# Feed-forward projections of a float32 transformer block with high and low input side by side in one 512-column operand

## What is computed

```python
def conv_ffn(x, w_up, conv_w, conv_b, w_down):      # x 256 x 1024, w_up 1024 x 5632, w_down 2816 x 1024
    u = x @ w_up
    ...
    up = jnp.pad(u, ((0, 0), (half, half), (0, 0)))
    c = conv_b
    for j in range(CONV_W):                          # CONV_W = 3, half = 1
        c = c + conv_w[j] * up[:, j:j + s]
    g, val = c[..., :FFN_HIDDEN], c[..., FFN_HIDDEN:]
    return (jax.nn.gelu(g) * val) @ w_down
```

## Time and profile before

| | |
|---|---|
| Median of 3 runs | 1061.26 us (1060.95 to 1061.63) |
| Profiled execution | span of 1058.9 us from the first to the last instruction |
| Busy over the span | TensorE 97%, VectorE 63%, ScalarE 53%, GpSimd 39% |
| Chain that ended last | TensorE 89% of the span, VectorE 4%, GpSimd 2%, ScalarE 2% |
| Two feed-forwards | 127.44 to 306.00 us and 451.04 to 626.68 us |

### The profile page before, as it was taken

How to read it: one execution, slowest core, us unless ns; L and a number is a source line. 1 busy time by engine, 2 the same in 40 slices (tenths; PEclk the granted TensorE clock), 3 DMA queues, 4 the chain that set the end, 5 groups by cost and what they waited for, 6 DMA issues and landing times.

```text
span 1058.9 us, 21783 instructions
## 1 busy us (share of the span) xinstructions
PE 1032.1 (97%) x8214; PEld 948.2 (90%) x8214; DVE 669.7 (63%) x1102; ACT 556.9 (53%) x1010; POOL 414.2 (39%) x281
## 2 busy tenths in 40 slices
PE   9899999999999999899999999999999999999997
PEld 7799699999988998699999997899999999999996
DVE  4555767677666666776776756766676555554445
ACT  5455665555555554756555566644443355554443
POOL 1000234433352334334333454865754375533331
PEclk9999999999999999999999999999999999999999
DMA  8333466665543544266656534233213244446551
GB/s 327 122 116 129 134 216 187 197 196 173 172 173 104 162 134 144 98 217 196 198 178 205 171 102 158 102 121 114 87 61 120 81 138 152 150 138 217 190 179 48
DMA packets 45993, 161.75 MB, mean 153 GB/s; under 512 B 5233, under 2 KB 5489, under 8 KB 45809
## 3 DMA queue, kind: packets, MB, share of 16 engines
q1 hardware_dynamic: 44784, 156.79, 45.3%
q0 software_dynamic: 1152, 4.19, 1.2%
HBM read 159.91 MB, written 1.05 MB: 152 GB/s over the span
## 4 chain that ended last, share of the span: by engine, by line
PE 89%; DVE 4%; POOL 2%; ACT 2%; issue 1%; DMA 1%; DVEq 0%; SPq 0%; ACTq 0%
PE work L400 14%; PE work L402 14%; PE work L401 14%; PE work L1777 9%; PE acc L400 6%; PE acc L401 6%; PE acc L402 5%; PE work L2499 4%; PE work L2511 3%; PE acc L2511 2%; POOL low L369 1%; PE acc L2028 1%; PE acc L2042 1%; PE acc L2044 1%; PE work L992 1%
## 5 line engine op out<-in xcount | busy, mean ns | idle before, releaser
L369 DVE TENSOR_TENSOR low<-raw,high 128x1024 fp32r<-128x1024 f32 (+2 forms) x185 | 273.7, 1487 | 160.9 <-ACT high L357 160.7
L369 POOL TENSOR_TENSOR low<-raw,high 128x1024 fp32r<-128x1024 f32 x108 | 263.1, 2440 | 286.1 <-ACT high L357 283.6
L357 ACT ACTIVATE high<-raw 128x1024 fp32r<-128x1024 f32 (+2 forms) x293 | 299.7, 1031 | 41.4 <-DMA raw<-in_w_out 25.0
L400 PE MATMUL work<-xh,high 128*128 128x256 f32 (+1 forms) x1032 | 289.9, 281 | 1.8 <-DVE v_sb L1469 1.7
L401 PE MATMUL work<-xl,high 128*128 128x256 f32 (+1 forms) x1032 | 287.9, 279 | 0.0
L402 PE MATMUL work<-xh,low 128*128 128x256 f32 (+1 forms) x1032 | 287.8, 279 | 0.0
L400 PEld LDWEIGHTS work<-xh,high 128*128 128x128 f32 (+1 forms) x1032 | 193.2, 187 | 8.7 <-issue 6.6
L401 PEld LDWEIGHTS work<-xl,high 128*128 128x128 f32 (+1 forms) x1032 | 193.3, 187 | 1.7
L402 PEld LDWEIGHTS work<-xh,low 128*128 128x128 f32 (+1 forms) x1032 | 193.3, 187 | 0.2
L1227 POOL TENSOR_TENSOR h<-gelu,cv 128x256 f32<-128x256 f32 x44 | 50.6, 1149 | 198.7 <-ACT gelu L1148 87.9
L1777 PE MATMUL work<-xh,high 128*128 128x256 f32 x256 | 76.7, 300 | 0.0
(11 more groups left out here) (393 smaller groups left out, 2197.3 us busy)
## 6 DMA issues: line engine op xcount, KB each, us to landing
raw<-in_w_ffn SPq DMA_DIRECT2D x132, 512.0 KB, 4.3
raw<-in_w_out SPq DMA_DIRECT2D x39, 512.0 KB, 4.1
raw<-in_w_att SPq DMA_DIRECT2D x32, 512.0 KB, 4.0
raw<-in_w_diff SPq DMA_DIRECT2D x31, 512.0 KB, 4.3
raw<-in_w_gdn SPq DMA_DIRECT2D x24, 512.0 KB, 4.0
raw<-in_w_mla SPq DMA_DIRECT2D x8, 512.0 KB, 3.6
raw<-in_w_gdnz SPq DMA_DIRECT2D x8, 512.0 KB, 3.6
raw<-in_w_mla SPq DMA_DIRECT2D x8, 384.0 KB, 3.1
```

What stands on the lines that cost most here:

```text
L357: act.activation(high[k][:, 0:w], raw[k][:, 0:w], ACT.Copy).then_inc(high_done[k], 1)
L369: eng.tensor_tensor(low[k][:, 0:w], raw[k][:, 0:w], high[k][:, 0:w], ALU.subtract).then_inc(low_done[k], 1)
L400: pe.matmul(out, lhs[0], rhs[0], start=start, stop=False)
```

## The change

The two input tensors become one, `xx`, with `xh` and `xl` as its halves. In the feed-forward's projections the two matmuls with the high weights become one of 512 columns, which writes high x high into columns 0 to 255 of a bank and high x low into columns 256 to 511; the matmul with the low weights adds to the first half. The two halves of a bank then have to be summed: ScalarE copies the second half to a new tile (`up_g` or `up_v`), VectorE adds the first half to it, and the middle tap and the outer taps read that sum from SBUF instead of PSUM. TensorE may write a bank again after the sum, no longer after the last tap. The high and low parts of slots 0, 1 and 2 move behind the copy and the sum of the bank that follows; that of slot 3 keeps its place. Other stages are as before, except for the counts of the semaphores that they share.

```diff
-    xh = sb("xh", [P, KB, TOK], F32R)
-    xl = sb("xl", [P, KB, TOK], F32R)
+    xx = sb("xx", [P, 2, KB, TOK], F32R)
+    xh, xl = xx[:, 0], xx[:, 1]
...
+    def project_pair(pe, bank, k, blocks=KB, arriving=None):
+
+        for b in range(blocks):
+            if arriving is not None and b % 4 == 0:
+                pe.wait_ge(n_["xl"], 4 * arriving + 2 + b // 2)
+            hi, lo = wslot(k, b * P, b * P + P)
+            pe.matmul(bank, hi, xx[:, :, b, :], start=(b == 0), stop=False)
+            last = pe.matmul(bank[:, 0:TOK], lo, xh[:, b, :], start=False, stop=(b == blocks - 1))
+        return last
...
-                    pe.wait_ge(f[j]["g_tap"] if gate else f[j]["v_tap"], 2 * (i + done))
+                    pe.wait_ge(f[j]["g_sum_tap"] if gate else f[j]["v_sum_tap"], 3 * (i + done) - 2)
...
-                project_t(pe, W[bank][:, 0:TOK], bank, arriving=2 * layer + 1 if first else None).then_inc(used[bank], 1)
+                project_pair(pe, W[bank], bank, arriving=2 * layer + 1 if first else None).then_inc(used[bank], 1)
...
                 act.wait_ge(used[bank], p.base[bank] + i + 1)
+                if not (isinstance(i, int) and i + done == 0):
+                    act.wait_ge(summed, 3 * (i + done))
+                act.activation(u[:], W[bank][:, TOK:2 * TOK], ACT.Copy).then_inc(made, 1)
+                if bank and not (late and value):
+                    refill(split, p, bank - 1, i)
+                act.wait_ge(summed, 3 * (i + done) + 1)
                 if value and not (isinstance(i, int) and i + done == 0):
                     act.wait_ge(s["h32"], i + done)
-                act.activation((cg, cv)[value][j][:], W[bank][:, 0:TOK], ACT.Identity,
+                act.activation((cg, cv)[value][j][:], u[:], ACT.Identity,
                                scale=ffn_taps(layer, i, j, value, 1, 0),
-                               bias=ffn_taps(layer, i, j, value, 3, 0)).then_inc((s["g_mid"], s["v_mid"])[value], 1)
-                if not late:
+                               bias=ffn_taps(layer, i, j, value, 3, 0)).then_inc(made, 1)
+                if bank == 3 and not late:
                     refill(split, p, bank, i)
...
-                dve.wait_ge(mid, i + done + 1)
-                dve.scalar_tensor_tensor(c[:, 1:TOK], W[bank][:, 0:TOK - 1], ffn_taps(layer, i, j, value, 0, 0),
+                dve.wait_ge(mid, 2 * (i + done) + 1)
+                dve.tensor_tensor(u[:], W[bank][:, 0:TOK], u[:], ALU.add).then_inc(tap, 1)
+                if bank and not (bank == 3 and last_step):
+                    refill(split, p, bank - 1, i)
+                dve.wait_ge(mid, 2 * (i + done) + 2)
+                dve.scalar_tensor_tensor(c[:, 1:TOK], u[:, 0:TOK - 1], ffn_taps(layer, i, j, value, 0, 0),
                                          c[:, 1:TOK], ALU.mult, ALU.add).then_inc(tap, 1)
...
-                if not (j and last_step):
-                    refill(split, p, bank, i)
```

More of the change, by code:

```diff
@@ L1081, in mla_dve @@
         over(dve, HEADS, head, 2)
-    f = [sems(f"f{j}", "g_mid v_mid g_tap v_tap gelu h32 hh hl") for j in range(2)]
+    f = [sems(f"f{j}", "g_copy_mid v_copy_mid g_sum_tap v_sum_tap gelu h32 hh hl") for j in range(2)]
+    up_g = [sb(f"up_g{j}", [P, TOK]) for j in range(2)]
+    up_v = [sb(f"up_v{j}", [P, TOK]) for j in range(2)]
     cg = [sb(f"cg{j}", [P, TOK]) for j in range(2)]
@@ L1138, in block @@
                 bank, s = 2 * j + value, f[j]
+                u = (up_g, up_v)[value][j]
+                made, summed = (s["g_copy_mid"], s["v_copy_mid"])[value], (s["g_sum_tap"], s["v_sum_tap"])[value]
                 act.wait_ge(used[bank], p.base[bank] + i + 1)
+                if not (isinstance(i, int) and i + done == 0):
[4 more added lines that the diff above has]
+                act.wait_ge(summed, 3 * (i + done) + 1)
                 if value and not (isinstance(i, int) and i + done == 0):
                     act.wait_ge(s["h32"], i + done)
-                act.activation((cg, cv)[value][j][:], W[bank][:, 0:TOK], ACT.Identity,
+                act.activation((cg, cv)[value][j][:], u[:], ACT.Identity,
                                scale=ffn_taps(layer, i, j, value, 1, 0),
-                               bias=ffn_taps(layer, i, j, value, 3, 0)).then_inc((s["g_mid"], s["v_mid"])[value], 1)
-                if not late:
+                               bias=ffn_taps(layer, i, j, value, 3, 0)).then_inc(made, 1)
+                if bank == 3 and not late:
                     refill(split, p, bank, i)
-            act.wait_ge(f[j]["g_tap"], 2 * (i + done) + 2)
+            act.wait_ge(f[j]["g_sum_tap"], 3 * (i + done) + 3)
             act.activation(gelu[j][:], cg[j][:], ACT.Gelu_apprx_tanh).then_inc(f[j]["gelu"], 1)
@@ L1186, in block @@
                 bank, s = 2 * j + value, f[j]
-                mid, tap, c = (s["g_mid"], s["v_mid"])[value], (s["g_tap"], s["v_tap"])[value], (cg, cv)[value][j]
-                dve.wait_ge(mid, i + done + 1)
-                dve.scalar_tensor_tensor(c[:, 1:TOK], W[bank][:, 0:TOK - 1], ffn_taps(layer, i, j, value, 0, 0),
+                mid, tap, c = (s["g_copy_mid"], s["v_copy_mid"])[value], (s["g_sum_tap"], s["v_sum_tap"])[value], (cg, cv)[value][j]
+                u = (up_g, up_v)[value][j]
+                dve.wait_ge(mid, 2 * (i + done) + 1)
[4 more added lines that the diff above has]
+                dve.scalar_tensor_tensor(c[:, 1:TOK], u[:, 0:TOK - 1], ffn_taps(layer, i, j, value, 0, 0),
                                          c[:, 1:TOK], ALU.mult, ALU.add).then_inc(tap, 1)
-                dve.wait_ge(tap, 2 * (i + done) + 1)
-                dve.scalar_tensor_tensor(c[:, 0:TOK - 1], W[bank][:, 1:TOK], ffn_taps(layer, i, j, value, 2, 0),
+                dve.wait_ge(tap, 3 * (i + done) + 2)
+                dve.scalar_tensor_tensor(c[:, 0:TOK - 1], u[:, 1:TOK], ffn_taps(layer, i, j, value, 2, 0),
                                          c[:, 0:TOK - 1], ALU.mult, ALU.add).then_inc(tap, 1)
-                if not (j and last_step):
-                    refill(split, p, bank, i)
         def step(i):
@@ L1223, in hidden @@
             pool.wait_ge(s["gelu"], i + done + 1)
-            pool.wait_ge(s["v_tap"], 2 * (i + done) + 2)
+            pool.wait_ge(s["v_sum_tap"], 3 * (i + done) + 3)
             if not (isinstance(i, int) and i + done == 0):
@@ L2796, in att_pool @@
         head(HEADS - 1)
-    r_ = dict(tha=f[0]["g_mid"], thb=f[0]["v_mid"], mh=f[0]["hh"], ma=f[0]["g_tap"], mb=f[0]["v_tap"],
-              sum=f[1]["g_tap"], ml=f[1]["v_tap"])
-    ACT_SEEN, DVE_SEEN = 2 * FFN_STEPS, 4 * FFN_STEPS
+    r_ = dict(tha=f[0]["g_copy_mid"], thb=f[0]["v_copy_mid"], mh=f[0]["hh"], ma=f[0]["g_sum_tap"], mb=f[0]["v_sum_tap"],
+              sum=f[1]["g_sum_tap"], ml=f[1]["v_sum_tap"])
+    ACT_SEEN, DVE_SEEN, TANH_SEEN = 2 * FFN_STEPS, 6 * FFN_STEPS, 4 * FFN_STEPS
     tha, thb = sb("tha", [P, TOK]), sb("thb", [P, TOK])
@@ L2823, in group @@
             final = isinstance(i, int) and i == HEADS - 1
-            pe.wait_ge(r_["tha"], i + ACT_SEEN)
+            pe.wait_ge(r_["tha"], i + TANH_SEEN)
             out_project(pe, 0, i, xh, xl)
-            pe.wait_ge(r_["thb"], i + ACT_SEEN)
+            pe.wait_ge(r_["thb"], i + TANH_SEEN)
             out_project(pe, 1, i, xh, xl)
@@ L2876, in group @@
             for k, (s, th, out, ready) in enumerate(((r_["ma"], tha, mga, r_["tha"]), (r_["mb"], thb, mgb, r_["thb"]))):
-                dve.wait_ge(ready, i + 1 + ACT_SEEN)
+                dve.wait_ge(ready, i + 1 + TANH_SEEN)
                 dve.wait_ge(used[2 + k], ph["out"].base[2 + k] + i + 1)
```

## The result

| | before | after |
|---|---|---|
| Median, measured side by side | 1061.45 us | 1120.27 us (1119.15 to 1121.49) |
| Profiled execution, span | 1058.9 us | 1119.2 us |
| First layer, first projection to the residual's first part | 127.44 to 312.89 = 185.45 us | 128.34 to 342.73 = 214.39 us |
| Second layer, the same | 451.04 to 636.49 = 185.45 us | 481.29 to 696.74 = 215.45 us |

The change makes the kernel slower by a factor of 1.056, with a 95% interval of 1.054 to 1.057. Of the 60.3 us between the two spans 58.9 lie in the two feed-forwards, 28.9 and 30.0. Another 0.9 stand ahead of the first of them: from a low part early in the first stage on (it starts at 12.04 us against 11.14 before) all is 0.9 later. In the nine runs of the experiments, which do the same up to there, that low part starts anywhere from 11.08 to 12.16, so that is no effect of the change.

What follows compares the result with a forecast made beforehand. A ring of VectorE, GpSimd and ScalarE was to replace TensorE as bound, 18.80 us a step against 16.5. Layers adding 27.75 and 28.95 us, 56.7 on a span of 1058.9, plus 2.4, gave 1118; range 1096 to 1128.

Steps and rivals of the forecast that it cites:

- the ring: Closed round trip of VectorE, GpSimd and ScalarE in each loop step: 18.80 us after, against TensorE's 16.5; chance 0.75.
- Term 1: VectorE's low part of slot 4 to the next operation, with GpSimd's slot 3 in front as before: 3.20 us.
- Term 2: Sum of bank 0, then ScalarE's Identity, then the tap: 1.2 us, bounds 0.9 and 1.3.
- The two trips: Twice a step, last tap to h, hh, high part and low part: 0.09 + 2.17 us, 2.26 each.
- TensorE's saving: Feed-forward projections: 0.0054 us saved a block, 704 blocks, 3.8 us in all, not subtracted as TensorE isn't the bound.
- Step 0: Step ahead of the loop in each layer: four sums, slot 1's low part and one exposed handoff add 3.0 us.
- The last step: First layer, last contended low part to the closing matmuls: 11.75 us becomes 14.8, so +3.05; second layer about 1.2 more.
- the rival of the clock: TensorE's clock falls to 1.2 GHz ahead of the closing matmuls: +7 us for both layers, 1125 us; chance 0.10.
- The lower end of the ring's range: Handoffs of 0.9 and taps without 0.1 of register work each: step of 17.95 us, time 1100.
- The port: Taps with two SBUF inputs wait for GpSimd's low parts; without that, the two last steps some 5 us shorter, 1113.
- The cover: Rival: the ring stays under TensorE's 16.5 us a step and the 3.8 us are kept: 1059 us; chance 0.06.
- the race at slot 4: Rival: VectorE's low part of slot 4 starts before GpSimd's of slot 3: step 17.9, time 1102 us; chance 0.06.

Runs made afterwards that it cites:

- the swap of two ScalarE operations: Changed kernel with ScalarE making the high part of slot 4 ahead of hh of half 1 in the loop; 1084.50 us.
- TensorE kept busy: Changed kernel with matmuls on constants in TensorE's two waits in the last step of each layer; 1117.63 us.
- The run with the old places: Changed kernel with each slot split where it was before the change, behind its own bank's taps; 1174.51 us.

## Why the prediction was right, point by point

The median, 1120.27, lies 2.3 us above the forecast of 1118.0 and inside the range.

- **Who bounds.** As put: TensorE had 0.3 us to spare, and the ring takes over. Both single-part runs of TensorE and the swap of two ScalarE operations show it: the operand alone on the kernel before gains, undoing it after the change does nothing, and the swap gives back 36 us.
- **The step.** 18.97 us, against 18.80 as summed. Term 1, the contended low part, is 3.19 (262.98 to 266.17), as in 3.20. Term 2 was mis-sized: from the sum of bank 0 to its tap it is 1.42 us, not 1.2 and above its upper bound of 1.3, since the wait from the end of the sum is 1.01. I had put Identity at 0.56 with 0.22 around it; it lasts 0.60, so 0.41 are around it. The other three sums are 0.33 to 0.34 to the next operation instead of 0.37, 0.1 less together. The two trips are 2.24 and 2.31 against 2.26.
- **TensorE's saving** is about 0.004 us a block, not 0.0054, and hidden as I said.
- **TensorE's wait** was forecast as some 2 us in every step. In most of the loop it is 1.87 and 0.55 in turn: behind the longer one the down projection mostly runs at half the clock, 4.42 us instead of 2.82, and the wait of the step behind it is short. Where the clock stayed up, at 550.21, the next wait is 1.87 again. Ahead of the closing matmuls I had 5 to 7 us; it is 4.00 and 5.44.
- **Step 0** added 2.45 us and not 3.0 (128.34 to 152.08 after, 127.44 to 148.73 before).
- **The last step** grew less: 323.08 to 336.82 is 13.74 us against the 14.8 of the forecast in the first layer, and 14.80 (675.83 to 690.63) against 16.0 in the second.
- **Closing.** From the closing matmuls to the residual 5.91 us after and 4.34 before, +1.57 instead of the 0.6 for the later root, and my sum had nothing there for the clock. With TensorE kept busy the root alone is left, at +0.38, so the clock makes 1.19 of it. Here the rival of the clock came true beside the main case: 0.52 in that stretch, where it was 1.00. Its price was too high: I had +7 for both layers, and the filled ends gave back 2. The Trainium skill says that a long idle gap between bursts returns the clock to its lower level (TensorE: Matmul & The Clock Gate, section "Why this matters for your kernels"), and the trace agrees, after a wait of 4.00 us. In the loop 1.87 us were enough in most cases, as the last section shows.
- **Sum.** First layer 2.45 + (171.00 - 148.07) + 1.99 + 1.57 = 28.94, forecast 27.75; second 30.0, forecast 28.95. That the first comes within 1.2 us is in part luck: I had put the nine steps 1.8 too low and the closing 1.0, but step 0 0.55 too high and the last step 1.1. The remaining 1.4 of the 60.3 lie outside the feed-forwards, most of them ahead of the first.
- **The lower end of the ring's range.** The 17.95 doesn't follow from its terms: 0.3 for the handoff and 0.1 for each of the four pairs of taps make it 18.1. The median doesn't use it.
- **The port.** Taps with both inputs in SBUF do wait for GpSimd (2.24, 2.46, 1.91 us), taps from PSUM at the same place don't (0.48). What the Trainium skill has in SBUF — State Buffer, section "SBUF: two separate sides", agrees with the runs, also for taps.
- **The other rivals.** The cover didn't hold, and the race at slot 4 stayed as it was (3.27 us for that low part). It turned only when I moved the high part.
- **What I took for granted wrongly.** I counted slot 1's low part in the second half as a cost of the change. The run with the old places shows that without the move the change would have cost 54 us more.

## What to carry to other kernels

An engine that is busy 70% of a stage can still be its bound: look for the round trip that starts and ends on it, and count what is put into that ring at full price, and what stands beside it at nothing. Before taking work out of a ring, look whether the order of two operations on a third engine closes it; here one swap was worth 36 us, and with two the steps of the loop took the added work for nothing (16.60 us against 16.69 before). Where one engine's result goes to another and back, put a long independent operation between, and keep operands that share the stage with GpSimd work in PSUM.

## What the runs showed of the hardware that I had not expected

- TensorE's clock can fall already behind a wait of 1.87 us. The two loops have ten down projections of half 0 behind a wait of 1.87 to 1.93 us. In eight of them six to eight of the 12 matmuls stand 0.42 to 0.43 us apart, which is the level of 1.2 GHz; the one at 235.44 takes 4.42 us, with a granted clock of 0.61 over the stretch. The other two, at 311.34 and 550.21, stand behind the same 1.87 us and run wholly at full clock, 2.82 us. So do the eight behind 0.55 to 0.73 us and those of the last steps, behind 1.65 and 1.27. In the first layer of the kernel with each sum twice all nine behind 1.84 to 2.59 us fell. The length of the wait alone doesn't decide it, and what else does is open. The step doesn't notice, because TensorE isn't its bound. Three starts of that down projection:

```profile
216.48 0.47 PE L400 MATMUL acc<-high,hh 128*128 128x512 f32 x1 [0.55 <-POOL hl L1252]
...
235.44 0.47 PE L400 MATMUL acc<-high,hh 128*128 128x512 f32 x1 [1.87 <-POOL hl L1252]
...
311.34 0.47 PE L400 MATMUL acc<-high,hh 128*128 128x512 f32 x1 [1.87 <-POOL hl L1252]
```

- A 512-column matmul and a 256-column one in turn take 0.347 us, a little more than the 0.3452 that the two add up to at the pace of each in a row of its own kind (0.2283 and 0.1169).
